# A decoder layer's first projection unit: its weight split moved ahead of the copies of the rows, its halves in two banks, and products that nobody reads ahead of it

## The chip, the cores and the metric

The kernel runs on one core of one Trainium2 chip. The metric is the device time of one execution in microseconds (us): lower is better. Engines are named as in the profile: PE (TensorE), PEld (its weight loads), DVE (VectorE), ACT (ScalarE), POOL (GpSimd), SP (SyncE, which issues nearly all transfers here).

## The reference

A decoder layer over 256 tokens of width 1024, in float32. Only its first line matters for the change; the rest is named to show what follows it.

```python
h = rms_norm(x, norm_mix_g[l])                        # (256, 1024)
proj = jnp.einsum('bsd,dc->bsc', h, w_in[l])          # (1024, 3080) weights
fq, fk, fv, f_logit, mq, mk, mv = jnp.split(proj, splits, axis=-1)
...                                                    # two kinds of attention, 8 heads each
x = x + jnp.einsum('bsc,cd->bsd', mixed, w_out[l])
h = rms_norm(x, norm_ffn_g[l])
x = x + hierarchical_moe(h, ...)                       # 32 experts, 2 a token, 96 MB of weights
return rms_norm(x, norm_final_g)
```

## The kernel before, in words

The program is written engine by engine, each in its own block, with semaphores between them; the order on an engine is the order of the code. No scheduler moves anything.

**Start.** SP issues the loads in this order: the two row tiles of x (512 KB each), four small vectors, the forget gate's weights `wf`, then `w_in` in pieces: two units of 256 columns (1 MB each, line 341), then five blocks of 512 columns (2 MB each, line 350). ACT squares each row tile (line 816), DVE and POOL make its reciprocal root, DVE scales the tile into `xn` (line 1161), and PE transposes its eight 128x128 pieces into banks 4 to 7 (line 469). A bank holds two of the eight slices k of the depth 1024.

**Split in two parts.** Rows and weights are each split for the products: `hi` is the value rounded to the fast matmul format, `lo` is what is left. ACT copies a slice of the transposed rows to `h_hi` (line 861) and DVE makes `h_lo` from the same bank (line 1165). ACT rounds a unit's weights to `unit_hi` (`split_hi`, line 839) and DVE subtracts to get `unit_lo` (`split_lo`, line 1173). For the first unit alone the subtraction is shared: POOL makes the lower four slices (line 1085, semaphore `half_lo_ready`) and DVE the upper four. Both start on the same semaphore, `w_hi_ready`.

**Units.** There are twelve units of 256 columns. A unit is 48 products of 128x256, 24 for each half of 128 columns: eight slices of hi times hi, eight of hi weights with `h_lo`, eight of lo weights with `h_hi`. `unit(0)` and `unit(1)` come first (line 488), then the forget gate (line 573), units 2 to 11 with the attention between them, the output projection, the router, and then the experts in passes, two experts side by side. During the experts SP waits for a pass to release a buffer and then issues the next 1 MB weight loads (lines 360, 367 and 415).

**Banks.** Unit u writes bank u % 3, both halves in one bank, and ACT takes it with one copy of 512 columns (line 823). Bank 3 (`O_BANK`) is first written by the forget gate. The tile `cpart` is a piece of SBUF that DVE sets to zero at the very start (line 1155).

Of the kernel before, what the change touches and what calls it, by code (L numbers as in the profile page):

```python
# [24 lines left out]
P = 128  # L25
SEQ = 256
# [3 lines left out]
KD = D // P  # L30
# [33 lines left out]
def layer_program(nc, I, out):  # L64
# [4 lines left out]
    with ctx:  # L69
# [3 lines left out]
        def sem(name):  # L73
            return ctx.enter_context(nc.semaphore(name))
# [181 lines left out]
        O_BANK = 3  # L256
# [19 lines left out]
        tr_done, h_hi_ready, h_lo_ready = sem("tr_done"), sem("h_hi_ready"), sem("h_lo_ready")  # L276
        w_hi_ready, w_lo_ready, wf_hi_ready, wf_lo_ready = (sem(n) for n in ("w_hi_ready", "w_lo_ready", "wf_hi_ready", "wf_lo_ready"))
        pad_clear = sem("pad_clear")
        grp_done, act_took, dve_took = sem("grp_done"), sem("act_took"), sem("dve_took")
        ft_done, ss_done, sq_ready, half_lo_ready = (sem(n) for n in ("ft_done", "ss_done", "sq_ready", "half_lo_ready"))  # L280
        fz_ready, fa_ready, fl_ready, fc_ready = (sem(n) for n in ("fz_ready", "fa_ready", "fl_ready", "fc_ready"))
# [25 lines left out]
        def grp_bank(g):  # L307
            return bank[g % 3]

        def wait_bank_free(pe, g):  # L310

            if g >= 3:
                if g - 3 < G_OF:
                    pe.wait_ge(act_took, g - 2)
                else:
                    pe.wait_ge(dve_took, g - 3 - G_OF + 1)
# [138 lines left out]
        @block.tensor  # L456
        def _(pe):
            mm = nc.tensor.matmul
            pe.wait_ge(cst_in, 16)

            pe.wait_ge(gv_in, 64)
# [2 lines left out]
            for t in range(NT):  # L464
                pe.wait_ge(xn_ready, t + 1)
                for i in range(KD // 2):
                    for k in (2 * i, 2 * i + 1):
                        c = (k % 2) * SEQ + t * P
                        last = nc.tensor.transpose(bank[4 + i][:, c:c + P], xn[:, t, k * P:(k + 1) * P], ident)
                    if t == NT - 1:  # L470
                        last.then_inc(tr_done, 1)
            def unit(u, parts=(0, 1)):

                if parts[0] == 0:
                    wait_bank_free(pe, u)
                    pe.wait_ge(w_hi_ready, u + 1)
                hi, lo = unit_hi[unit_buf(u)], unit_lo[unit_buf(u)]
                for i in parts:
                    out = grp_bank(u)[:, i * UNIT:(i + 1) * UNIT]  # L480
                    if u < G_FV:
                        for n, (w, h) in enumerate(((hi, h_hi), (hi, h_lo), (lo, h_hi))):
                            if n == 2:
                                wait_split(pe, u)
                            for k in range(KD):
                                if u == 0 and i == 0 and n < 2:
                                    pe.wait_ge((h_hi_ready, h_lo_ready)[n], k + 1)
                                last = mm(out, w[:, k, i * P:(i + 1) * P], h[:, k, :], start=(n == 0 and k == 0), stop=(n == 2 and k == KD - 1))  # L488
                    else:
                        for n, (h, w) in enumerate(((h_hi, hi), (h_lo, hi), (h_hi, lo))):  # L490
                            if n == 2:
                                wait_split(pe, u)
                            for k in range(KD):
                                last = mm(out, h[:, k, i * P:(i + 1) * P], w[:, k, :], start=(n == 0 and k == 0), stop=(n == 2 and k == KD - 1))  # L494
                if parts[-1] == 1:
                    last.then_inc(grp_done, 1)
# [67 lines left out]
                    last.then_inc(grp_done, 1)  # L564

            pe.wait_ge(gcol_set, 1)
            unit(0)
            unit(1)

            pe.wait_ge(wf_lo_ready, 1)  # L570
# [227 lines left out]
        def _(act):  # L798
# [55 lines left out]
                took(g, mqk[:, w, :, c:c + UNIT], both_tiles(g))  # L854

            for k in range(KD):
                if k == KD // 2:
                    split_hi(0)
                act.wait_ge(tr_done, k // 2 + 1)  # L860
                A(h_hi[:, k, :], bank[4 + k // 2][:, (k % 2) * SEQ:(k % 2 + 1) * SEQ], ACT.Copy, scale=gcol[:, k:k + 1]).then_inc(h_hi_ready, 1)
            split_hi(1)
            act.wait_ge(wf_in, 16)
            nc.scalar.copy(wf_hi[:, :, :], wf).then_inc(wf_hi_ready, 1)
            take_qk(0)
            split_hi(2)
            take_qk(1)
            split_hi(3)
# [275 lines left out]
        def _(dve):  # L1144
# [7 lines left out]
                dve.wait_ge(dve_step, steps[0])  # L1152

            V.memset(onescol, 1.0).then_inc(ones_set, 1)
            V.memset(cpart, 0.0)

            for t in range(NT):
                dve.wait_ge(ssq_ready, t + 1)
                V.tensor_scalar(var[:, t:t + 1], ssq[:, t:t + 1], 1.0 / D, EPS, ALU.mult, ALU.add).then_inc(var_ready, 1)
                dve.wait_ge(pow_ready, t + 1)  # L1160
                V.tensor_scalar(xn[:, t, :], x[:, t, :], rstd[:, t:t + 1], None, ALU.mult).then_inc(xn_ready, 1)
            dve.wait_ge(gcol_set, 1)
            for k in range(KD):
                dve.wait_ge(h_hi_ready, 2 * (k // 2) + 2)
                V.scalar_tensor_tensor(out=h_lo[:, k, :], in0=bank[4 + k // 2][:, (k % 2) * SEQ:(k % 2 + 1) * SEQ], scalar=gcol[:, k:k + 1],
                                       in1=h_hi[:, k, :].bitcast(fp32), op0=ALU.mult, op1=ALU.subtract).then_inc(h_lo_ready, 1)

            def split_lo(u):

                dve.wait_ge(w_hi_ready, u + 1)  # L1170
# [1 line left out]
                k = slice(KD // 2 if u == 0 else 0, KD)  # L1172
                V.tensor_tensor(unit_lo[b][:, k, :], unit_src(u)[:, k, :], unit_hi[b][:, k, :].bitcast(fp32), ALU.subtract).then_inc(w_lo_ready, 1)  # L1173

            split_lo(0)
            split_lo(1)
            dve.wait_ge(wf_hi_ready, 1)
            V.tensor_tensor(wf_lo[:, :, :], wf, wf_hi[:, :, :].bitcast(fp32), ALU.subtract).then_inc(wf_lo_ready, 1)
# [330 lines left out]
```

## Time and profile before

| what | us |
|---|---|
| median of 3 runs | 364.67 (364.49 to 366.02) |
| the profiled execution | 363.79 |
| its span, first to last instruction | 361.6 |
| PE busy in the span | 312.5 (86%) |
| mean granted TensorE clock, as a share of 2.4 GHz | 0.978 |

The rows further down are all of the profiled execution, whose own time is 2.2 us above its span and 0.88 us below the median of the runs. Start times count from the first instruction.

### The profile page before, as it was taken

The page shows a single profiled execution, that of the slowest core. Times are in us where ns is not written, and L with a number is a line of the kernel's source. Part 1 is how long each engine was busy: PE and PEld are TensorE (multiplying, and loading weights), DVE is VectorE, ACT ScalarE, POOL GpSimd, SP SyncE. Part 2 cuts the span into 40 slices and gives each one's busy share as a digit, 9 for nine tenths or more (in the row PEclk, how much of TensorE's full clock was granted, in tenths as well). Part 3 has the DMA queues.
Part 4 walks back from the last instruction along what each step waited for, and adds up shares of the span by engine and source line. Part 5 has one row for each costly group of instructions (what it writes and reads, how often), then busy time and mean ns, then how long its engine had stood idle before and what let it go on. Part 6 is the DMA issues. An engine that isn't in the chain of part 4 may idle for free.

```text
span 361.6 us, 11575 instructions
## 1 busy us (share of the span) xinstructions
PE 312.5 (86%) x4740; PEld 240.3 (66%) x4741; DVE 163.9 (45%) x453; ACT 125.0 (35%) x307; POOL 42.7 (12%) x73
## 2 busy tenths in 40 slices
PE   1799999999999989889979898889999999766571
PEld 1699989889875545667657665657677777546250
DVE  2635545383353612774535344435555544341334
ACT  4726336545241426533313232312323323220223
POOL 1200000363402225620000000000000000000002
PEclk9899999999999999999989999999999999998997
DMA  8999795062729989489999999999999999999943
GB/s 254 352 386 387 263 392 239 3 237 112 280 81 400 314 353 387 160 304 348 418 414 357 418 418 414 416 418 410 423 412 421 418 415 423 410 424 416 414 175 116
DMA packets 32652, 121.17 MB, mean 335 GB/s; under 512 B 5497, under 2 KB 7825, under 8 KB 24689
## 3 DMA queue, kind: packets, MB, share of 16 engines
q1 hardware_dynamic: 32480, 120.65, 85.1%
q8 instruction: 21, 0.34, 0.4%
q10 hardware_dynamic: 144, 0.13, 0.1%
q14 instruction: 7, 0.05, 0.0%
HBM read 119.72 MB, written 1.05 MB: 334 GB/s over the span
## 4 chain that ended last, share of the span: by engine, by line
PE 68%; issue 8%; DMA 7%; DVE 4%; DVEq 4%; SPq 4%; ACT 3%; POOL 0%; POOLq 0%; ACTq 0%
PE bank L494 13%; PE bank L770 8%; PE bank L738 7%; PE bank L698 7%; PE bank L561 7%; PE bank L488 7%; DMA spare<-in_w_up_dram 6%; PE bank L705 4%; SPq L360 2%; PE bank L508 2%; PE bank L759 2%; ACT yb L1016 2%; PE bank L523 1%; DVEq L1431 1%; DMA ring<-in_norm_ffn_g_dram 1%
## 5 line engine op out<-in xcount | busy, mean ns | idle before, releaser
L738 PE MATMUL bank<-ring,hT 128*32 128x128 f32 x1664 | 53.2, 279 | 12.7 <-issue 4.7
L738 PEld LDWEIGHTS bank<-ring,hT 128*32 128x32 f32 x1664 | 46.1, 112 | 23.8 <-issue 23.3
L1426 DVE SCALAR_TENSOR_TENSOR yb<-bank,pp,yb 64x512 fp32r<-64x512 f32 x36 | 27.0, 749 | 45.8 <-ACT yb L1016 45.2
L1173 DVE TENSOR_TENSOR unit_lo<-ring,unit_hi 128x2048 fp32r<-128x2048 f32 (+1 forms) x12 | 26.3, 2207 | 32.6 <-ACT unit_hi L839 32.6
L698 PE MATMUL bank<-pp,qk 128*128 128x64 bf16 x912 | 30.6, 194 | 8.2 <-issue 4.7
L698 PEld LDWEIGHTS bank<-pp,qk 128*128 128x128 bf16 x912 | 28.1, 98 | 13.4 <-issue 7.4
L1016 ACT ACTIVATE yb<-bank,pp 64x512 fp32r<-64x512 f32 x36 | 24.6, 683 | 28.9 <-PE bank L770 28.4
L1078 POOL TENSOR_TENSOR stats<-stats 128x1 f32<-128x1 f32 (+1 forms) x7 | 4.6, 664 | 219.8 <-DVE stats L1457 199.7
L561 PE MATMUL bank<-ring,qk 128*128 128x512 f32 (+1 forms) x72 | 29.9, 551 | 0.0
L770 PE MATMUL bank<-ring,pp 128*32 128x512 f32 x208 | 25.0, 598 | 0.0
L705 PE MATMUL bank<-yb,selT 128*128 128x512 f32 x76 | 23.3, 428 | 1.7 <-DVE yb L1426 1.6
L738 PE MATMUL bank<-work,hT 128*32 128x128 f32 x320 | 19.4, 273 | 4.8 <-DMA spare<-in_w_up_dram 2.9
L738 PEld LDWEIGHTS bank<-work,hT 128*32 128x32 f32 x320 | 17.0, 110 | 9.0 <-issue 8.9
L839 ACT CAST unit_hi<-ring 128x2048 fp32r<-128x2048 f32 x12 | 22.8, 1911 | 0.0
L1368 DVE TENSOR_TENSOR hT<-bank,stats 128x256 f32<-128x256 f32 x38 | 14.5, 420 | 14.8 <-PE bank L698 14.8
L1006 ACT ACTIVATE pp<-bank,stats 128x128 f32<-128x128 f32 x18 | 6.6, 368 | 41.0 <-PE bank L738 41.0
L738 PE MATMUL bank<-spare,hT 128*32 128x128 f32 x320 | 19.5, 274 | 0.0
L561 PEld LDWEIGHTS bank<-ring,qk 128*128 128x128 f32 x72 | 12.7, 190 | 9.9 <-issue 9.7
L1008 ACT COPY pp<-bank 128x128 f32<-128x128 f32 x18 | 4.8, 266 | 41.2 <-PE bank L761 41.2
L1398 DVE TENSOR_SCALAR pp<-cf,qk 128x64 f32<-128x64 f32 x76 | 18.6, 309 | 0.0
L494 PE MATMUL bank<-unit_hi,h_hi 128*128 128x256 f32 x128 | 18.4, 287 | 0.0
L494 PE MATMUL bank<-unit_hi,h_lo 128*128 128x256 f32 x128 | 18.0, 283 | 0.0
(197 smaller groups left out, 513.6 us busy)
## 6 DMA issues: line engine op xcount, KB each, us to landing
ring<-in_w_up_dram SPq DMA_DIRECT2D x24, 1024.0 KB, 19.1
ring<-in_w_down_dram SPq DMA_DIRECT2D x24, 1024.0 KB, 19.1
ring<-in_w_gate_dram SPq DMA_DIRECT2D x22, 1024.0 KB, 16.9
ring<-in_w_in_dram SPq DMA_DIRECT2D x5, 2048.0 KB, 19.4
ring<-in_w_out_dram SPq DMA_DIRECT2D x4, 1024.0 KB, 8.5
spare<-in_w_gate_dram SPq DMA_DIRECT2D x4, 1024.0 KB, 19.0
spare<-in_w_up_dram SPq DMA_DIRECT2D x4, 1024.0 KB, 19.7
work<-in_w_gate_dram SPq DMA_DIRECT2D x4, 1024.0 KB, 16.8
```

Source lines behind the costliest of these rows:

```text
L488: last = mm(out, w[:, k, i * P:(i + 1) * P], h[:, k, :], start=(n == 0 and k == 0), stop=(n == 2 and k == KD - 1))
L494: last = mm(out, h[:, k, i * P:(i + 1) * P], w[:, k, :], start=(n == 0 and k == 0), stop=(n == 2 and k == KD - 1))
L561: last = mm(grp_bank(g)[:, 0:w], oT[:, j, t * P:(t + 1) * P], w_o[:, group, c // HALF, k, c % HALF:c % HALF + w], start=(k == 0), stop=(k ...
L698: last = mm(dst[:, k * CP:(k + 1) * CP], hs[i][:, t, k, :], selb[:, t, :], start=(t == 0 and i == 0), stop=(t == NT - 1 and i == 2))
L705: last = mm(acc[t][half][:, :], selT[:, t * P:(t + 1) * P], yb[half][:, :], start=False, stop=final)
L738: last = mm(p_gu[b:b + CAP, w * P:(w + 1) * P], hg[:, k, CAP * e:CAP * (e + 1)], w_gu[at[e]][:, w, k, h, :], start=(k == 0), stop=(k == KD ...
L770: last = mm(p_y[b:b + CAP, :], actT[:, CP * f + CAP * e:CP * f + CAP * (e + 1)], w_dn[at[e]][:, f, h * HALF:(h + 1) * HALF], start=(f == 0 ...
L839: nc.scalar.copy(unit_hi[unit_buf(u)][:, :, :], unit_src(u)).then_inc(w_hi_ready, 1)
L1016: A(yb[half][rows, :], p_y[rows, :], ACT.Copy, scale=wcol[rows, :]).then_inc(y_hi_ready, 1)
L1173: V.tensor_tensor(unit_lo[b][:, k, :], unit_src(u)[:, k, :], unit_hi[b][:, k, :].bitcast(fp32), ALU.subtract).then_inc(w_lo_ready, 1)
L1398: last = V.tensor_scalar(selw[:, t, :].rearrange("p (h e c) -> p e h c", h=2, e=2)[:, e], slots.rearrange("p (h c) -> p h c", h=2), at, we ...
L1426: V.scalar_tensor_tensor(out=yb[half][rest, :], in0=p_y[rows, :], scalar=wcol[rows, :], in1=yb[half][rows, :].bitcast(fp32), op0=ALU.mult, ...
```

## The change

Four things are done to the start of the program; nothing behind unit 1 is edited, except that PE waits before unit 2, which writes bank 2, until ACT has emptied it.

```diff
+        WARM = 20
+        first_bank = [bank[0], bank[2]]
         def wait_bank_free(pe, g):
+            if g == 2:
+                pe.wait_ge(act_took, 1)
...
         @block.tensor
+            pe.wait_ge(zero_set, 1)
+            for i in range(WARM):
+                mm(bank[O_BANK][:, 0:SEQ], cpart[:, 0:P], cpart, start=True, stop=True)
             pe.wait_ge(cst_in, 16)
...
+            def first_unit():
+                pe.wait_ge(w_hi_ready, 1)
+                hi, lo = unit_hi[0], unit_lo[0]
+                for n, (w, h) in enumerate(((hi, h_hi), (lo, h_hi), (hi, h_lo))):
+                    if n == 1:
+                        wait_split(pe, 0)
+                    for k in range(KD):
+                        if n != 1:
+                            pe.wait_ge(h_hi_ready if n == 0 else h_lo_ready, k + 1)
+                        for i in range(2):
+                            last = mm(first_bank[i][:, 0:SEQ], w[:, k, i * P:(i + 1) * P], h[:, k, :],
+                                      start=(n == 0 and k == 0), stop=(n == 2 and k == KD - 1))
+                last.then_inc(grp_done, 1)
...
-            unit(0)
+            first_unit()
             unit(1)
...
         @block.scalar
+            split_hi(0)
             for k in range(KD):
-                if k == KD // 2:
-                    split_hi(0)
                 act.wait_ge(tr_done, k // 2 + 1)
                 A(h_hi[:, k, :], bank[4 + k // 2][:, (k % 2) * SEQ:(k % 2 + 1) * SEQ], ACT.Copy, scale=gcol[:, k:k + 1]).then_inc(h_hi_ready, 1)
...
-            take_qk(0)
+            act.wait_ge(grp_done, 1)
+            for i in range(2):
+                last = nc.scalar.copy(qT[:, i, :], first_bank[i][:, 0:SEQ])
+            last.then_inc(act_took, 1)
...
         @block.vector
-            V.memset(cpart, 0.0)
+            V.memset(cpart, 0.0).then_inc(zero_set, 1)
...
             dve.wait_ge(gcol_set, 1)
+            split_lo(0)
             for k in range(KD):
                 dve.wait_ge(h_hi_ready, 2 * (k // 2) + 2)
                 V.scalar_tensor_tensor(out=h_lo[:, k, :], in0=bank[4 + k // 2][:, (k % 2) * SEQ:(k % 2 + 1) * SEQ], scalar=gcol[:, k:k + 1],
                                        in1=h_hi[:, k, :].bitcast(fp32), op0=ALU.mult, op1=ALU.subtract).then_inc(h_lo_ready, 1)
-            split_lo(0)
             split_lo(1)
```

On PE, the first unit of before stands in these rows behind the transposes; `unit_hi_53` and `unit_lo_57` are the first unit's weight parts, `unit_hi_54` is the second unit's.

```order
L488 MATMUL bank<-h_hi,unit_hi_53 128x256 [waits h_hi_ready,w_hi_ready,gcol_set]
L488 MATMUL bank<-h_hi,unit_hi_53 128x256 [waits h_hi_ready] x7
L488 MATMUL bank<-h_lo,unit_hi_53 128x256 [waits h_lo_ready] x8
L488 MATMUL bank<-h_hi,unit_lo_57 128x256 [waits w_lo_ready,half_lo_ready]
L488 MATMUL bank<-h_hi,unit_lo_57 128x256 x7
L488 MATMUL bank<-h_hi,unit_hi_53 128x256 x8
L488 MATMUL bank<-h_lo,unit_hi_53 128x256 x8
L488 MATMUL bank<-h_hi,unit_lo_57 128x256 [waits w_lo_ready,half_lo_ready]
L488 MATMUL bank<-h_hi,unit_lo_57 128x256 x7
L488 MATMUL bank<-h_hi,unit_hi_54 128x256 [waits w_hi_ready]
```

With the change the same place reads as follows, from the last pair of hi times hi products to the first pair with `h_lo` (seven more hi pairs stand ahead, the first of which also waits for `w_hi_ready`, and seven more `h_lo` pairs behind).

```order
L494 MATMUL bank<-h_hi,unit_hi_53 128x256 [waits h_hi_ready]
L494 MATMUL bank<-h_hi,unit_hi_53 128x256
L494 MATMUL bank<-h_hi,unit_lo_57 128x256 [waits w_lo_ready,half_lo_ready]
L494 MATMUL bank<-h_hi,unit_lo_57 128x256 x15
L494 MATMUL bank<-h_lo,unit_hi_53 128x256 [waits h_lo_ready]
L494 MATMUL bank<-h_lo,unit_hi_53 128x256
```

So each slice of `h_hi` now feeds two products as it comes, 16 products need the rows' hi parts alone, and the wait for the weights' lo parts stands behind those 16 instead of behind 8 hi and 8 `h_lo` products; 32 products are left behind that wait in either order.

On ACT, the rows of before from the copy of the gains to the first unit's result:

```order
L818 COPY gcol<-bank 128x24 [waits gcol_t]
L861 ACTIVATE h_hi<-bank,gcol 128x256 [waits tr_done,gcol_set]
L861 ACTIVATE h_hi<-bank,gcol 128x256 [waits tr_done] x3
L839 CAST unit_hi_53<-ring 128x2048 [waits unit_in0]
L861 ACTIVATE h_hi<-bank,gcol 128x256 [waits tr_done] x4
L839 CAST unit_hi_54<-ring 128x2048 [waits unit_in1]
L864 CAST wf_hi<-ring 128x64 [waits wf_in]
L823 COPY qk<-bank 128x512 [waits grp_done]
```

The same stretch of ACT with the change:

```order
L842 COPY gcol<-bank 128x24 [waits gcol_t]
L863 CAST unit_hi_53<-ring 128x2048 [waits unit_in0,gcol_set]
L884 ACTIVATE h_hi<-bank,gcol 128x256 [waits tr_done] x8
L863 CAST unit_hi_54<-ring 128x2048 [waits unit_in1]
L887 CAST wf_hi<-ring 128x64 [waits wf_in]
L890 COPY qk<-bank 128x256 [waits grp_done]
L890 COPY qk<-bank 128x256
```

The rounding of the first weights, which stood between the fourth and the fifth copy of the rows, now stands ahead of all eight.

On DVE, the rows of before around the first lo parts:

```order
L1161 TENSOR_SCALAR pp<-work,stats 128x1024 [waits pow_ready]
L1165 SCALAR_TENSOR_TENSOR h_lo<-bank,gcol,h_hi 128x256 [waits h_hi_ready,gcol_set]
L1165 SCALAR_TENSOR_TENSOR h_lo<-bank,gcol,h_hi 128x256 [waits h_hi_ready] x7
L1173 TENSOR_TENSOR unit_lo_57<-ring,unit_hi_53 128x1024 [waits w_hi_ready]
L1173 TENSOR_TENSOR unit_lo_58<-ring,unit_hi_54 128x2048 [waits w_hi_ready]
```

The same stretch of DVE with the change:

```order
L1187 TENSOR_SCALAR pp<-work,stats 128x1024 [waits pow_ready]
L1193 TENSOR_TENSOR unit_lo_57<-ring,unit_hi_53 128x1024 [waits w_hi_ready,gcol_set]
L1199 SCALAR_TENSOR_TENSOR h_lo<-bank,gcol,h_hi 128x256 [waits h_hi_ready] x8
L1193 TENSOR_TENSOR unit_lo_58<-ring,unit_hi_54 128x2048 [waits w_hi_ready]
L1204 TENSOR_TENSOR wf_lo<-ring,wf_hi 128x64 [waits wf_hi_ready]
```

DVE's half of the first weights' lo part moved ahead of the eight `h_lo` slices, so that it and POOL's half wait for nothing but the same `w_hi_ready`.

## Rows read from the trace of the kernel before

**Rows 1.** Pieces of the chain that ended last: start us, us, what.

```profile
7.61 3.67 PE bank L469 x16
11.29 2.28 issue
13.56 13.97 PE bank L488 x96
27.53 2.78 PE bank L573 x24
...
187.81 1.53 PE bank L705 x4
...
197.13 0.93 PE bank L705 x4
...
321.94 21.78 DMA spare<-in_w_up_dram
```

**Rows 2.** Timeline of the start: start us, us, engine, line, what, count, idle before it.

```profile
10.11 1.57 ACT L861 ACTIVATE h_hi<-bank,gcol 128x256 fp32r<-128x256 f32 x4 [2.31 <-PE bank L469]
11.55 1.91 ACT L839 CAST unit_hi<-ring 128x2048 fp32r<-128x2048 f32 x1
13.34 1.60 ACT L861 ACTIVATE h_hi<-bank,gcol 128x256 fp32r<-128x256 f32 x4
13.54 2.39 POOL L1085 TENSOR_TENSOR unit_lo<-ring,unit_hi 128x1024 fp32r<-128x1024 f32 x1 [5.29 <-ACT unit_hi L839]
14.24 1.66 DVE L1165 SCALAR_TENSOR_TENSOR h_lo<-bank,gcol,h_hi 128x256 fp32r<-128x256 f32 x4 [1.53 <-ACT h_hi L861]
15.37 1.91 PE L488 MATMUL bank<-h_lo,unit_hi 128*128 128x256 f32 x8
17.18 1.72 PE L488 MATMUL bank<-h_hi,unit_lo 128*128 128x256 f32 x8
18.74 1.12 PE L488 MATMUL bank<-h_hi,unit_hi 128*128 128x256 f32 x8
21.61 1.12 PE L488 MATMUL bank<-h_hi,unit_hi 128*128 128x256 f32 x8
```

**Rows 3.** Landings, of lines 341 (two loads) and 350 (five): issued, and us to landing.

```profile
L341 SPq DMA_DIRECT2D ring<-in_w_in_dram x2: 582/1232/1883, 3.5 to 4.1; - x2
DMA to landing us min/median/max: 6.5/7.8/9.0
L350 SPq DMA_DIRECT2D ring<-in_w_in_dram x5: 437/4008/6372, 9.3 to 21.7; - x5
DMA to landing us min/median/max: 10.7/19.4/20.8
```

**Rows 4.** POOL and DVE alone, 69.5 to 75.5 us; then line 1067's durations (ns min/median/max).

```profile
72.64 2.45 POOL L1067 TENSOR_TENSOR ring<-qk 128x256 f32<-128x256 f32 x1 [0.24 <-ACT qk L903]
72.32 2.29 DVE L1173 TENSOR_TENSOR unit_lo<-ring,unit_hi 128x2048 fp32r<-128x2048 f32 x1 [3.74 <-ACT unit_hi L839]
L1067 POOL TENSOR_TENSOR ring<-qk x6: 609/614/2446, 72.6 to 117.4; 128x256 f32<-128x256 f32 x6
L1173 DVE TENSOR_TENSOR unit_lo<-ring,unit_hi x12: 1220/2292/2326, 15.8 to 89.4; 128x2048 fp32r<-128x2048 f32 x11, 128x1024 fp32r<-128x1024 f32 x1
```

**Rows 5.** Stretches: us, PE busy (count), PE clock granted, DMA share, GB/s.

```profile
15.00:16.00 1.00, 1.00 (x5) 0.50 1.03 385
19.00:20.00 1.00, 1.00 (x11) 1.00 1.05 387
148.00:152.00 4.00, 2.82 (x16) 1.00 0.19 41
184.00:188.00 4.00, 3.41 (x56) 0.70 1.00 418
192.00:196.00 4.00, 4.00 (x140) 1.00 0.78 280
```

**Rows 6.** Longest waits of SP's queue: for whom, us in total, times, longest.

```profile
SPq L360 <- PE bank L738: 23.6, 13, 13.0
```

More of the change, by code:

```diff
@@ L278, in layer_program @@
         pad_clear = sem("pad_clear")
+        zero_set = sem("zero_set")
         grp_done, act_took, dve_took = sem("grp_done"), sem("act_took"), sem("dve_took")
@@ L485, in unit @@
                             for k in range(KD):
-                                if u == 0 and i == 0 and n < 2:
-                                    pe.wait_ge((h_hi_ready, h_lo_ready)[n], k + 1)
                                 last = mm(out, w[:, k, i * P:(i + 1) * P], h[:, k, :], start=(n == 0 and k == 0), stop=(n == 2 and k == KD - 1))
@@ L1161, in _ @@
                 V.tensor_scalar(xn[:, t, :], x[:, t, :], rstd[:, t:t + 1], None, ALU.mult).then_inc(xn_ready, 1)
[L1162 to L1166, printed above, removed]
             def split_lo(u):
@@ L1173, in split_lo @@
                 V.tensor_tensor(unit_lo[b][:, k, :], unit_src(u)[:, k, :], unit_hi[b][:, k, :].bitcast(fp32), ALU.subtract).then_inc(w_lo_ready, 1)
+            dve.wait_ge(gcol_set, 1)
             split_lo(0)
+            for k in range(KD):
+                dve.wait_ge(h_hi_ready, 2 * (k // 2) + 2)
+                V.scalar_tensor_tensor(out=h_lo[:, k, :], in0=bank[4 + k // 2][:, (k % 2) * SEQ:(k % 2 + 1) * SEQ], scalar=gcol[:, k:k + 1],
+                                       in1=h_hi[:, k, :].bitcast(fp32), op0=ALU.mult, op1=ALU.subtract).then_inc(h_lo_ready, 1)
             split_lo(1)
```

## The prediction

> **What bounds the kernel now.** I read the chain of waits first, since it says which stretch of the start is worth anything. It runs on PE almost without a break from the transposes on, and the only long piece of it that is no engine's work is the last weight load, 21.78 us from its issue to its landing at 343.7 [rows 1]. At the start the chain has one hole: PE ends the transposes at 11.3, stands still for 2.28 us, and then runs 96 products of line 488 without a stop that the chain names, 13.97 us [rows 1]. At full clock 96 would take 11.5: eight products last 1.12 us there, which is seven steps and a last one of 0.28, so a step is 0.12 [rows 2]. So the first unit has two places to gain: the hole, and 2.5 us of slack inside.
>
> The timeline shows both. ACT copies four slices of the rows, rounds the first weights from 11.55, and only when they are done, at about 13.48, can PE begin; then it copies the other four, and PE follows at the copies' pace of 0.36 us (four in 1.60: three steps and 0.51). The eight `h_lo` products from 15.37 take 1.91 and the next eight from 17.18 take 1.72, steps of 0.21 instead of 0.12 [rows 2]; the stretch view has the granted clock at 0.50 there, that is 1.2 GHz, and back at 1.00 at 19 [rows 5]. PE had stood still ahead of 13.5 and worked in short pieces behind it. The second unit starts at 21.61 [rows 2]. This is the mark of the whole calculation: how much earlier does it start?
>
> **Step 1, the weights first.** The first unit's 1 MB is issued at 3.5 and lands 6.5 later, at 10.0 [rows 3]. That is the moment at which ACT now starts its first copy (10.11 [rows 2]), so the moved rounding starts at 10.05. In the rows the next copy starts 1.79 behind its start (13.34 less 11.55), and the semaphore comes at 1.92; so hi weights at 11.97, and eight copies from 11.84 on in steps of 0.36: the first is ready at 11.84 + 0.51 = 12.35, the last at 11.84 + 7 x 0.36 + 0.51 = 14.87. Before, the last was ready at 14.94 by the same sum (13.34 + 1.60). ACT's work is only put in another order, so the rows are not ready sooner; what changes is that PE can follow the copies from the first on. What ACT had as cover, its copies between the landing and 11.55, is gone: from here on the landing of the first weights is on the path, one for one.
>
> **Step 2, both halves at each slice.** PE starts at 12.4 and has two products, 0.24 us, for every 0.36. Its last pair starts at 14.9 and is through at 15.15. At half clock the pair would take 0.43, so 16 would take 3.4 and end at 15.8: PE then sets the pace, and the bound is 0.65 worse.
>
> **Step 3, the lo weights.** Now 32 products are left, all behind the wait for both halves of the lo part. DVE's half took 1.2 us in the rows of its line, POOL's 2.39 [rows 2, 4]. Side by side they would be ready at 12.0 + 2.4 = 14.4 and hidden behind the pairs. But the trace has one place where such a pair meets. At 72.32 DVE starts a subtraction with both inputs in SBUF, for 2.29 us; POOL starts a product from SBUF 0.3 later and takes 2.45 where the same form takes 0.61, so it ended at 75.09, 0.48 behind DVE's end at 74.61 [rows 4]. It did next to nothing until DVE was done. Against that, POOL ran its half of before beside the `h_lo` instructions in 2.39 [rows 2], and these have one input in a bank. The change makes the bad pair: both halves start on one semaphore at 12.0. One waits for the other, whichever is first: 12.0 + 1.2 + 2.39 = 15.6. PE restarted 0.14 behind the last release before (DVE's half, from 15.82 for 1.22, to 17.18 [rows 2, 4]), so it goes on at 15.74, and stands still for some 0.6.
> The Trainium skill says the same as a rule (SBUF — State Buffer, section Who interferes with whom): a VectorE instruction with two SBUF inputs and a GpSimd instruction that reads SBUF use one port pair, and the second to start blocks until the first is done. By that rule as by the row the sum is 15.74; without it, it would be 15.15. The trace agrees, with 2.45 against 0.61.
>
> **Step 4, the rest of the unit.** 32 steps of 0.12 are 3.84, so the second unit starts at 15.74 + 3.84 = 19.58 instead of 21.61: 2.03 earlier. In parts: the restart behind the lo wait moves from 17.18 to 15.74, 1.44, with 32 products behind it both times; and the eight from 17.18 took 1.56 to the next eight at 18.74, instead of 0.96, which gives 0.60 if the clock holds. I take it that it does: PE works from 12.4 with two thirds of its time filled, where it had stood still until 13.56. Bounds of the start: 1.44 if there is nothing to win back from the clock, 2.62 if the two halves don't block (21.61 less 15.15 + 3.84 = 18.99). I take 2.03, with the row that shows the block and the clock of this trace.
>
> **What costs nothing, and under which cover.** The 20 unread products wait only for DVE's second instruction; at 0.21 each they take 4.3 us, and the transposes don't start before 7.6 [rows 1]. Whether they make the transposes faster has no effect: the last transposes end at 11.3 [rows 1] even at the slow pace, and ACT needs the first pair of slices at 11.84. `h_lo` on DVE starts behind its 1.2 us, at 13.2, and goes in steps of 0.39, limited by the copies: all eight are ready by 16.4, the first is needed at 15.74 + 1.92 = 17.7. If POOL is the first of the two, DVE's half ends at 15.6 and `h_lo` 0 at 16.1: still in time. The second unit's lo part is done 2.3 us behind 16.8, needed at 21.5. ACT's two copies of 256 columns instead of one of 512 cost it some 0.15, eight us ahead of unit 2, which starts at 30.3 less 2.0 [rows 1]; its block of weights lands at 9.3 + 10.7 = 20.0 and the last block at 21.7 + 20.8 = 42.5 [rows 3], both ahead of their use. The new wait ahead of unit 2 is for copies that ended 8 us before.
>
> **Does the start carry to the end?** The end is set by the weight stream, which is full to the last load. But a stream that has run dry starts again when PE releases a buffer, and it runs dry at 148 to 152 (41 GB/s) and again for part of 192 to 196 (280 GB/s) [rows 5]. SP's longest wait for PE in that part, 13.0 us, ends just there [rows 6]. From 196 on it is full. Everything between 42 and 193 is thus released by PE, and moves with it. So the sum is 363.79 - 2.03 = 361.8 for the profiled execution. That one lies 0.88 below the median of the runs, so for the median 364.67 - 2.03 = 362.6. Since part of the runs may not have the 0.60 in them, I say 362.7.
>
> **The rivals.**
> - *Only the wait is won* (2 in 10): the clock's 0.60 is not there in most executions, or comes back as a slow stretch elsewhere in the unit. 1.44 is left: 363.2, within 0.5%.
> - *The halves don't block* (1 in 10): the start gives 2.62, so 362.1. For it speaks only that both are short; the row at 72.6 speaks against.
> - *The stream takes it* (1 in 10): the gaps of 148 to 152 and 192 to 196 close, and the end waits for bytes alone; 364.7, no change. Against it: the first gap alone is nearly four us, more than the shift.
> - *The clock among the experts falls otherwise* (1 in 10): there the granted clock is 0.70 in 184 to 188, and four products of line 705 take 1.53 instead of 0.93 [rows 1, 5], on the way to the release at 193. Another position of such a stretch gives or takes at most 4 x 0.30 = 1.2 there: 361.4 to 363.8.
> - *Slower* (under 1 in 10): the first weights land late. ACT now waits for them with all the rows behind it. Break even is a landing at 12.05 instead of 10.0; if they land with the unit behind them, at 4.1 + 9.0 = 13.1 [rows 3], the start loses 3.1 and wins 2.0: 365.8; it is slower by 0.5% from 13.9 on. For it: both loads share the queues. Against: before, they landed 3.1 apart.
> - *The unread products do nothing.* This is what I expect of them, and it costs nothing.
>
> **How the numbers follow.** 0.5% is 1.8 us, about what a measurement of this kernel can tell from no change. The likeliest case (5 in 10), 2.03 with a spread of some 0.4 for the landing and the clock, lies just over that bound, and two thirds of it count as faster; with the unblocked case and half of the clock case that makes 0.50. The rest of these, the case of the wait alone and that of the stream make 0.43 for no difference, the last rival and what I have not thought of 0.07 for slower. The range goes from 361.3 (unblocked, with luck in the clock among the experts) to 364.4 (nearly all lost on the way).
>
> **What would show it.** In the changed kernel's trace: the rounding of the first weights on ACT starts at the landing, near 10.0; PE's first pair at 12.4 and pairs every 0.36; on POOL the half takes 3.6 instead of 2.4, or DVE's half that much longer, and PE stands still from 15.15 to 15.7; granted clock 1.00 from 15 to 19; the second unit at 19.6; the gap in the stream near 191 instead of 193. The prediction is wrong if the first weights land later than 10.5, if the clock is at 0.50 behind 15, or if the last landing stays at 343.7.

## The result and the profile after

The changed kernel takes 367.0 us in the median (twelve executions), the kernel before beside it 364.2. The ratio of their times is 1.0065, with a 95% interval of 1.0041 to 1.0090: **slower by 0.65%, 2.4 us**, where 362.7 and a gain of 2.0 had been predicted. (All ratios here and below leave out executions over 1.5% above their kernel's fastest: four of these twelve, from 370.8 up, and in e10 three, one of them of 1,044 us.) The profiled execution took 366.56, its span is 364.7 and its mean granted clock 0.970; before they were 363.79, 361.6 and 0.978.

The start did what was predicted. The timeline of the changed kernel, as in [rows 2]:

```profile
9.94 1.90 ACT L863 CAST unit_hi<-ring 128x2048 fp32r<-128x2048 f32 x1 [2.37 <-DMA ring<-in_w_in_dram]
11.75 3.02 ACT L884 ACTIVATE h_hi<-bank,gcol 128x256 fp32r<-128x256 f32 x8
11.92 2.38 POOL L1111 TENSOR_TENSOR unit_lo<-ring,unit_hi 128x1024 fp32r<-128x1024 f32 x1 [3.52 <-ACT unit_hi L863]
11.95 3.43 DVE L1193 TENSOR_TENSOR unit_lo<-ring,unit_hi 128x1024 fp32r<-128x1024 f32 x1 [2.77 <-ACT unit_hi L863]
12.36 2.97 PE L494 MATMUL bank<-h_hi,unit_hi 128*128 128x256 f32 x16 [1.15 <-ACT h_hi L884]
15.52 2.15 PE L494 MATMUL bank<-h_hi,unit_lo 128*128 128x256 f32 x16 [0.20 <-DVE unit_lo L1193]
17.51 2.08 PE L494 MATMUL bank<-h_lo,unit_hi 128*128 128x256 f32 x16
19.43 1.12 PE L512 MATMUL bank<-h_hi,unit_hi 128*128 128x256 f32 x8
```

The second unit's first product, the last row, starts at 19.43, not at 21.61 as in [rows 2]: 2.18 earlier (2.03 predicted). So the profiled execution lacks nearly 5 us against its forecast (366.56 for 361.8), and they were lost later. The chain of waits (start us, us, what) says where:

```profile
3.48 6.38 DMA ring<-in_w_in_dram
9.94 1.91 ACT unit_hi L863
11.95 3.44 DVE unit_lo L1193
15.52 4.07 PE bank L494 x32
19.59 5.76 PE bank L512 x48
...
150.94 4.35 PE bank L684 x6
...
264.44 6.53 issue
270.97 3.58 PE bank L762 x64
```

Two pieces are new. The second of them is long: PE ends a pass at 264.44 and starts the next one at 270.97, and in between it waits for nothing that the profile shows. The last weight load, 21.78 us of the chain before [rows 1], is not in it any more: from 270.97 on the chain goes over PE, with short steps of ACT and DVE between the passes, and over no load. Stretches of the changed kernel (columns: us, PE busy, PEld, DVE, ACT, POOL with counts, PE clock granted, DMA share, GB/s):

```profile
152.00:156.00 4.00, 4.00 (x12) 1.49 (x10) 2.33 (x14) 0.00 (x0) 1.57 (x6) 0.64 0.65 254
...
264.00:268.00 4.00, 0.44 (x6) 0.00 (x0) 1.50 (x2) 1.36 (x2) 0.00 (x0) 0.94 1.00 398
268.00:272.00 4.00, 1.03 (x20) 1.06 (x24) 0.53 (x3) 0.00 (x0) 0.00 (x0) 0.50 1.04 420
```

In 264 to 272 PE is busy for 1.5 of 8 us; the granted clock drops to 0.50 during the stop and is still there when PE goes on (0.50 in 268 to 272), while the DMA engines stay full: it is not data that is late. What is late is on another queue. Transfers of the stretch 255 to 345 us by queue (packets, MB, share of 16 engines), first the changed kernel, then the kernel before:

```profile
q1 hardware_dynamic: 6603, 37.30, 101.0%
q8 instruction: 9, 0.15, 0.7%
```

```profile
q1 hardware_dynamic: 6678, 37.57, 101.7%
```

`q8 instruction` carries PE's code, in packets of 16 KB; that it is PE's shows in e4 and e7 below, where 240 more PE instructions bring one packet more in all, 23 instead of 22. Before, PE fetches none in this stretch; the changed kernel fetches nine, the first at 264.68, where PE has just stopped, the second at 266.37, then one every 6 to 8 us until 310.6. The place is the end of the first of three iterations of the expert loop, where PE jumps back to the loop's first instruction (its branch is at 262.87; the next ones at 313.82 and 352.33). Before, with branches at 260.15, 298.58 and 349.31, the same jump costs a gap of 0.72 us.

From these times the loss can be laid out. The start's 2.19 us are carried by SP's issues up to 151. Then 1.4 is lost to a stretch of half clock over the router's products (150.94 to 155.3, six of them in 4.35 us, and 0.64 in the row of 152 to 156), 1.35 more by SP's issue at 193 (nearly all of it a pause of PE in the products of line 794 at 176: 3.19 us from 175.39, where before they took 1.90), and at the jump PE is 2.7 late.

The 2.2 us between 193 and the jump stand in two more pauses that the kernel before doesn't have, 1.2 at 220 and 0.9 at 252.7; each comes right behind a code packet (217.70 and 250.78), but no run isolates them, and other traces with the stop reach the jump earlier (e2 at 260.41, e3 at 260.91).

The second iteration, with the stop, takes 50.9 us instead of 38.4, 12.5 more: 5.8 at the jump (6.53 for 0.72), 2.3 and 1.2 in stops at 286.35 and 299.68, 1.6 for 64 products at half clock (3.58 for 1.96), and the rest in pieces. The third takes 38.5 instead of 50.7, 12.2 less. The sum of 2.7, 12.5 and -12.2 is 3.0, by which the end comes later.

What the third iteration has less is waiting for weights. PE's longest waits in 260 to 350 (for whom, us in total, times, longest), before and after:

```profile
PE bank L738 <- DMA ring<-in_w_up_dram: 4.6, 2, 2.9
PE bank L738 <- DMA ring<-in_w_gate_dram: 3.1, 1, 3.1
PE bank L738 <- DMA spare<-in_w_up_dram: 2.9, 1, 2.9
PE bank L738 <- DMA spare<-in_w_gate_dram: 1.6, 1, 1.6
PE bank L738 <- issue: 1.4, 2, 0.7
```

```profile
PE bank L762 <- issue: 10.4, 7, 6.5
...
PE bank L722 <- issue: 1.2, 1, 1.2
```

The 12.2 us of waits for loads are gone, all of them: they were PE's slack against the stream, and the wait for code and the half clock behind it have used them up. Without that slack PE sets the end and not the last load, which lands 1.6 us later than before (345.3 for 343.7).

### The profile page after: what moved, and what is told of

Same layout as the page of the kernel before. It is cut to its first block, busy times and chain, and to the rows that moved or that the text cites. A ratio compares the mean times of both kernels' runs of the same rounds, so it can differ in the third digit from the quotient of the medians.

```text
span 364.7 us, 11616 instructions
## 1 busy us (share of the span) xinstructions
PE 320.8 (88%) x4760; PEld 242.4 (66%) x4761; DVE 166.0 (46%) x453; ACT 125.0 (34%) x308; POOL 42.7 (12%) x73
## 4 chain that ended last, share of the span: by engine, by line
PE 73%; issue 10%; DVE 4%; ACT 4%; DVEq 4%; DMA 2%; SPq 1%; POOLq 0%; POOL 0%; ACTq 0%
PE bank L518 13%; PE bank L794 10%; PE bank L762 9%; PE bank L722 8%; PE bank L585 7%; PE bank L729 5%; PE bank L512 5%; PE bank L783 2%; PE bank L532 2%; ACT yb L1042 2%; DMA ring<-in_w_in_dram 2%; PE bank L684 1%; PE bank L547 1%; DVEq L1457 1%; DVEq L1456 1%
## 5 line engine op out<-in xcount | busy, mean ns | idle before, releaser
L1193 DVE TENSOR_TENSOR unit_lo<-ring,unit_hi 128x2048 fp32r<-128x2048 f32 (+1 forms) x12 | 28.6, 2390 | 31.7 <-ACT unit_hi L863 31.7
L722 PEld LDWEIGHTS bank<-pp,qk 128*128 128x128 bf16 x912 | 28.6, 99 | 12.5 <-DVE pp L1373 6.7
L794 PE MATMUL bank<-ring,pp 128*32 128x512 f32 x208 | 28.1, 599 | 0.5 <-issue 0.5
## 6 DMA issues: line engine op xcount, KB each, us to landing
ring<-in_w_down_dram SPq DMA_DIRECT2D x24, 1024.0 KB, 16.9
```

The lines of the kernel that those rows point to most:

```text
L722: last = mm(dst[:, k * CP:(k + 1) * CP], hs[i][:, t, k, :], selb[:, t, :], start=(t == 0 and i == 0), stop=(t == NT - 1 and i == 2))
L794: last = mm(p_y[b:b + CAP, :], actT[:, CP * f + CAP * e:CP * f + CAP * (e + 1)], w_dn[at[e]][:, f, h * HALF:(h + 1) * HALF], start=(f == 0 ...
```

## The experiments

Rivals: the time of the products or the clock after them; the two-bank order or the earlier start, which changes what PE meets at the loop; a part of the start that costs.

**e1_no_products.** The changed kernel without its unread products.

```diff
-            pe.wait_ge(zero_set, 1)
-            for i in range(WARM):
-                mm(bank[O_BANK][:, 0:SEQ], cpart[:, 0:P], cpart, start=True, stop=True)
```

> The changed kernel without the 20 unread products and the wait ahead of them; all else as changed. Theory A (code loading): the 20 products and their weight loads are 40 instructions ahead of the expert loop, and they push the loop over one more loaded block of code, so that its first jump back waits for code (6.5 us at 264 in the changed kernel, and nine more code packets on queue 8). Without them the count of instructions ahead of the loop is that of before: no code packets between 251 and 350 us, no stop of over 3 us near 264, and the start's 2.0 us reach the end: 361.5 to 362.8. Rival B (clock): the start's 2.2 us shift makes PE stand still at a worse moment in the router, 0.50 granted at 151.5, and that eats it: the stretch is still there and the time is 363.5 to 366. Rival C (start): the unread products keep the clock up for the first unit, and without them it runs at half clock: the second unit starts at 20.5 or later instead of 19.4.

Measured: 362.09 beside 363.79, ratio 0.9955 (0.9927 to 0.9984): **faster**. The jump back in its chain, and no row of `q8` between 255 and 345:

```profile
260.75 0.71 issue
```

The rest of the change is thus worth 0.45%, and the products cost 1.0065 against 0.9955, 1.1% or 4.0 us. The interval of the 0.45% goes from 0.6 to 2.7 us. In its profiled execution, which at 364.39 is the second slowest of the twelve, PE ran at half clock up to about 16.9 (its products go in steps of 0.21 until there), and the second unit started 1.42 earlier than before rather than 2.18:

```profile
12.35 3.75 PE L491 MATMUL bank<-h_hi,unit_hi 128*128 128x256 f32 x16 [1.01 <-ACT h_hi L881]
15.90 2.53 PE L491 MATMUL bank<-h_hi,unit_lo 128*128 128x256 f32 x16
...
20.19 1.12 PE L509 MATMUL bank<-h_hi,unit_hi 128*128 128x256 f32 x8
```

**e2_before_products.** The kernel before with the 20 products and nothing else of the change.

```diff
+            pe.wait_ge(zero_set, 1)
+            for i in range(20):
+                mm(bank[O_BANK][:, 0:SEQ], cpart[:, 0:P], cpart, start=True, stop=True)
             pe.wait_ge(cst_in, 16)
...
-            V.memset(cpart, 0.0)
+            V.memset(cpart, 0.0).then_inc(zero_set, 1)
```

> The kernel before with the 20 unread products alone, in the same place, behind DVE's zeroing. Theory A (code loading): the first jump back of the expert loop stops PE for some 6 us and nine more code packets are loaded, so 366.5 to 369, 2 to 5 us slower than before. Rivals B (clock in the router) and C (products help the start): no such stop, 363 to 364.5, since the start is otherwise the old one and the products lie in idle time.

Measured: ratio 1.0125 (1.0081 to 1.0170). The stop is there, and so are nine code packets (0.15 MB of `q8` between 255 and 345). In its chain:

```profile
261.98 6.58 issue
```

Neither the new order nor the earlier start is needed for it. In this trace the second unit started 0.40 later than before, at 22.01: the products brought no clock either.

**e3_20_small.** The same number of unread products, each as small as can be: they take hardly any time of PE's array, but as many instructions.

```diff
-                mm(bank[O_BANK][:, 0:SEQ], cpart[:, 0:P], cpart, start=True, stop=True)
+                mm(bank[O_BANK][0:32, 0:1], cpart[:, 0:32], cpart[:, 0:1], start=True, stop=True)
```

> The changed kernel with its 20 unread products made small (32 weight columns, one column streamed), so that they take a few tenths of their time but are still 40 instructions. Theory A (code loading): as slow as the changed kernel, 365 to 368, with the stop at the first jump back. A theory by which the products' work (clock, power) is what costs: as fast as without them, 361.5 to 363.

Measured: ratio 1.0063 (1.0032 to 1.0094), the same as the change, with the stop:

```profile
262.48 6.68 issue
```

They were over at 1.76 us. The products' work plays no part; it is enough that they are 40 instructions.

**e4_120_small.** 120 small products instead of 20: 240 instructions.

```diff
-            for i in range(WARM):
-                mm(bank[O_BANK][:, 0:SEQ], cpart[:, 0:P], cpart, start=True, stop=True)
+            for i in range(120):
+                mm(bank[O_BANK][0:32, 0:1], cpart[:, 0:32], cpart[:, 0:1], start=True, stop=True)
```

> The changed kernel with 120 small unread products in place of the 20, which is 240 instructions instead of 40. The extra code packets are of 16 KB, 256 instructions of 64 bytes. Theory A (code loading): 240 is nearly a whole packet, so the loop lies in its packets as without any of them, 16 instructions further ahead: no stop at the jump, no packets between 251 and 350 us, 361.5 to 363.5 although there are six times as many instructions (they may delay the transposes by up to 1 us, of which little reaches the end). A theory by which any added instruction costs: slower than the kernel with 20, over 366.

Measured: ratio 0.9995 (0.9973 to 1.0017); no stop (a gap of 0.71 at 259.70) and no code packet in 255 to 345. Six times as many instructions and no stop: it is the place of the code, not its amount. The gain of e1 wasn't there in full, though. Its chain starts like this:

```profile
3.48 7.52 DMA ring<-in_w_in_dram
...
11.08 1.90 ACT unit_hi L863
...
13.50 0.55 PE bank L494
```

The first weights land at 11.00 instead of 9.86, and PE's first product starts at 13.50 instead of 12.36: 1.14 and 1.14, one for one. A code packet runs at 5.53, and SP's two issues take 3.43 us instead of 2.55; that this packet delays the weights is a guess that no run isolates, and e12, without a packet there, has 2.91.

**e7_20_and_100.** The changed kernel's 20 products and 100 small ones behind them, again 240 instructions.

```diff
+            for i in range(100):
+                mm(bank[O_BANK][0:32, 0:1], cpart[:, 0:32], cpart[:, 0:1], start=True, stop=True)
             pe.wait_ge(cst_in, 16)
```

> The changed kernel with its 20 unread products and 100 small ones behind them: 240 instructions ahead, as with 120 small ones. Theory A: no stop at the jump. This leaves the one question what the 20 do for the clock: if keeping PE at work from 1.0 to 5.2 us helps the first unit, this is 0.5 us or more faster than 120 small ones (363.6), 362.5 to 363; if the clock at 12 to 17 us does not depend on them, 363.2 to 364.

Measured: ratio 0.9975 (0.9954 to 0.9995), no stop. The jump back in its chain:

```profile
257.51 0.72 issue
```

The change as it is, with more useless instructions in it, is 0.9% faster than without them.

**e6_behind.** The kernel before with 20 small unread products behind the loop, at the end of PE's program.

```diff
+            for i in range(20):
+                mm(p_gu[0:32, 0:1], cb[:, 0:32], cb[:, 0:1], start=True, stop=True)
```

> The kernel before with 20 small unread products (40 instructions) at the very end of PE's program, behind the expert loop, where the last results are being scaled. Theory A (where the loop lies in the code packets): the same 40 instructions cost nothing here, no code packets between 251 and 350 us, within 0.3% of before (some 2 us of them lie beside the last steps of DVE and ACT). If the number of instructions in all were what counts, 365.5 to 368.

Measured: ratio 0.9991 (0.9965 to 1.0017), no stop (0.72 at 260.60). Behind the loop the 40 instructions cost nothing.

**e8_10_products** and **e11_16_products.** The changed kernel with fewer products, one execution each.

```diff
-        WARM = 20
+        WARM = 10
```

> The changed kernel with 10 unread products, 20 instructions instead of 40. Read for the code packets alone: theory A has a step somewhere between 0 and 40 instructions, so this trace has either none of the nine packets between 251 and 350 us and no stop near 262, or all of them and a stop of 6 to 7 us, and nothing between. A cost that grows with the instructions would give a stop of about half, 3 us.

```diff
-        WARM = 20
+        WARM = 16
```

> The changed kernel with 16 unread products instead of 20, that is 32 instructions ahead instead of 40 (10 products, 20 instructions, left the expert loop without a stop). If the cost is a step set by where the loop's code lies, it is there in whole, 6.5 us and nine code packets, or not at all; a cost that grows with the instructions would show a stop of 2 to 5 us. The run tells on which side of 32 instructions the step lies.

Measured: 363.98 and 365.55. The jump back in the chain of the first and of the second:

```profile
264.05 0.71 issue
```

```profile
261.46 6.72 issue
```

20 instructions: no stop, no packet. 32: the whole stop and nine packets. 40: the same. The stop is a step; what it costs in whole time, two single executions can't say.

**e5_one_lo.** e1 with the shared port's block taken away: DVE makes all eight slices of the first unit's lo part, and POOL's instruction and the wait for it are out.

```diff
-            nc.gpsimd.tensor_tensor(unit_lo[0][:, k, :], unit_src(0)[:, k, :], unit_hi[0][:, k, :].bitcast(fp32),
-                                    ALU.subtract).then_inc(half_lo_ready, 1)
...
-                k = slice(KD // 2 if u == 0 else 0, KD)
+                k = slice(0, KD)
```

> The kernel without the unread products, with DVE making all eight slices of the first unit's lo weights and POOL none; its wait is gone with its instruction. Theory of the shared port (two SBUF inputs on DVE beside a POOL instruction that reads SBUF): in the changed kernel DVE's half lasts 3.43 us instead of 1.2 because it waits for POOL's; alone, DVE needs 2.3 for the double work, so the lo weights are ready at 14.3 instead of 15.4, before PE has done the 16 hi products, and PE goes through without the stop of 0.4: the second unit starts 0.35 to 0.45 earlier, 361.2 to 362 in all. If the long DVE instruction came from something else (the transfers, the copies on ACT), it would stay over 3 us for 2048 elements, the lo weights would come later than now, and the time would be 362 to 363.

Measured: ratio 0.9955 (0.9926 to 0.9983). DVE's subtractions (ns min/median/max), and PE's rows:

```profile
L1184 DVE TENSOR_TENSOR unit_lo<-ring,unit_hi x12: 2281/2292/2328, 11.9 to 86.7; 128x2048 fp32r<-128x2048 f32 x12
```

```profile
12.31 2.96 PE L489 MATMUL bank<-h_hi,unit_hi 128*128 128x256 f32 x16 [1.12 <-ACT h_hi L879]
15.11 2.07 PE L489 MATMUL bank<-h_hi,unit_lo 128*128 128x256 f32 x16
18.94 1.12 PE L507 MATMUL bank<-h_hi,unit_hi 128*128 128x256 f32 x8
```

Alone, DVE does the double work in 2.29 us, where its half took 3.43 beside POOL's. PE no longer stops ahead of the lo products, and the second unit starts at 18.94, 0.49 earlier than in the changed kernel. In the whole time the 0.49 can't be told from e1.

**e9_weights_first.** The kernel before with the order on ACT and DVE alone.

```diff
+            split_hi(0)
             for k in range(KD):
-                if k == KD // 2:
-                    split_hi(0)
...
             dve.wait_ge(gcol_set, 1)
+            split_lo(0)
             for k in range(KD):
...
-            split_lo(0)
             split_lo(1)
```

> The kernel before with one part of the change alone: on ACT the first weights are rounded ahead of the eight copies of the rows, and on DVE the half of their lo part stands ahead of h_lo. PE's program is untouched, and there are no unread products, so no theory expects a stop at the first jump back of the expert loop. By the changed kernel's trace DVE's half then ends at about 15.4 us beside POOL's half, h_lo begins there, and its eight slices come every 0.39 from about 15.9 to 18.6. PE's first half of the unit meets them behind its eight hi products, which follow the copies until about 15.1: it ends its h_lo products at 18.8, and has 8 + 24 products of 0.12 left, 3.8 us: the second unit at 22.6 instead of 21.61, 1.0 later. If the order on ACT and DVE alone carried the gain, it would start some 2 us earlier instead. Whole time: 364.5 to 365 by the first, 362 by the second.

Measured: ratio 1.0106 (1.0072 to 1.0140): slower, as by the first reading, and by more. Its timeline:

```profile
11.95 3.41 DVE L1166 TENSOR_TENSOR unit_lo<-ring,unit_hi 128x1024 fp32r<-128x1024 f32 x1 [2.92 <-ACT unit_hi L839]
12.36 3.04 PE L488 MATMUL bank<-h_hi,unit_hi 128*128 128x256 f32 x8 [1.08 <-ACT h_hi L860]
15.81 3.32 PE L488 MATMUL bank<-h_lo,unit_hi 128*128 128x256 f32 x8 [0.41 <-DVE h_lo L1172]
...
20.64 1.84 PE L488 MATMUL bank<-h_hi,unit_hi 128*128 128x256 f32 x8
24.23 1.12 PE L488 MATMUL bank<-h_hi,unit_hi 128*128 128x256 f32 x8
```

The block on DVE pushes `h_lo` behind 15.3, and in the old order PE needs `h_lo` right behind the hi products. The eight `h_lo` products end near 18.9 as expected; then the steps are 0.21 up to 22.3, which adds 1.6, and the second unit starts at 24.23, 2.6 later than before. The whole loses 3.9 us, 1.3 more than that; this trace also has the granted clock at 0.50 from 155 to 159 and from 189.5 to 196, and no run says whose doing that is.

**e10_pairs_only.** The other part alone: two banks and the new order on PE, ACT and DVE as before, no unread products.

```diff
-            split_hi(0)
             for k in range(KD):
+                if k == KD // 2:
+                    split_hi(0)
...
-            split_lo(0)
             for k in range(KD):
...
+            split_lo(0)
             split_lo(1)
```

> The other part alone: both halves side by side in two banks and PE's new order of products, with ACT and DVE in the order of before (rounding between the fourth and the fifth copy, DVE's half behind h_lo), and no unread products, so no stop in the expert loop. PE starts at 13.5 as before, is through with its 16 hi products at 15.3, waits for DVE's half until 17.2 (15.82 and 1.22, and 0.14), and then has 32 products at 0.12, 3.84 us: the second unit at 21.0 instead of 21.61, 0.6 earlier. If the pairs alone carried the gain, it would start at 19.6. Whole time: 363.2 to 363.6 by the first, 362 by the second.

Measured: ratio 1.0035 (0.9996 to 1.0074), no gain, and not clearly a loss. Its timeline, and one stretch of it:

```profile
13.41 2.92 PE L491 MATMUL bank<-h_hi,unit_hi 128*128 128x256 f32 x16 [2.28 <-issue]
17.02 3.75 PE L491 MATMUL bank<-h_hi,unit_lo 128*128 128x256 f32 x16 [0.69 <-DVE unit_lo L1191]
...
22.79 1.12 PE L509 MATMUL bank<-h_hi,unit_hi 128*128 128x256 f32 x8
```

The restart at 17.02 was expected at 17.2. But the granted clock is at 0.50 from 15 to 21 in the stretches of this trace, and the 32 products behind the wait take 5.8 us and not 3.84; the second unit starts 1.2 later than before, not 0.6 earlier. How much of the whole time is the order's and how much this clock's, the run doesn't tell apart. Neither part gains alone: weights first needs PE's new order, to have work that doesn't ask for `h_lo`, and PE's new order needs the weights first, to start before 13.4.

**e12_one_lo_10.** e5 with 10 unread products, 20 instructions.

```diff
+            pe.wait_ge(zero_set, 1)
+            for i in range(10):
+                mm(bank[O_BANK][:, 0:SEQ], cpart[:, 0:P], cpart, start=True, stop=True)
```

> The candidate: the changed kernel with 10 unread products instead of 20, and the whole lo part of the first weights made by DVE (POOL's instruction and its wait are out). 10 products with their weight loads are 20 instructions, which left the loop's code where it does no harm, so no stop of PE at the first jump back (a gap of about 0.7 us). DVE's subtraction takes 2.3 us from 11.9, done at 14.2 as without the products. If the products do nothing but take instructions, the whole time is that of the same kernel without them, 0.9955 of before, 362.4 to 362.9. If they win clock in the first unit in most executions (up to 1.2 us, the difference between the starts of the runs so far), it is 0.992 to 0.994, 361.5 to 362. If 20 instructions move the loop badly in this program, it is 1.006 as for the change.

Measured: 362.14, ratio **0.9938** (0.9912 to 0.9964), faster than both kernels, with a gap of 0.71 at the jump. Its interval overlaps that of e5, so that the products win something is not shown; and in its profiled execution they didn't hold the clock (16 lo products in 2.70 us, the second unit at 20.73).

## Why the prediction was wrong

**The step that failed** is "What costs nothing, and under which cover". It asked only when the 20 products run and who waits for them, and there it was right. It didn't ask where their 40 instructions put the code behind them, and so put them at nothing. What stands in its place: they cost 4.0 us in the whole (e1 against the change), through a stop of 6.5 us at the loop's first jump back and shorter ones behind it. e2 shows that they alone do it, e3 that their time doesn't matter, e6 that it needs them ahead of the loop, e4, e7, e8 and e11 that it is a question of position. The Trainium skill (Runtime: NRT & Kernel Launch, Instruction fetch mechanics) bears on it: code comes in 16 KiB blocks of 256 instructions into a memory that has 128 KiB for PE, and a taken branch whose target isn't in the current window of two pages waits for a fetch.
The stop was not of the order of one fetch either: the first took 1.02 us, the second was fetched at 266.37, and PE went on at 270.97. My theory of a loop that lies over one packet more than PE keeps is not shown either, and the third iteration speaks against it: code that doesn't fit would be fetched in every iteration, but in the changed kernel the third, with the same code at the same place, fetched nothing (no packet between 310.57 and 351.36). Which packet the first jump waits for, and why 32 instructions are enough and 20 and 240 are not, the runs don't show beyond the position itself.

**"Does the start carry to the end?"** failed as well. It followed the weight stream alone, and took it for given that PE has slack against it. It has, 12.2 us of waits for loads behind the jump, and that is why a second iteration 12.5 us longer costs only 4.0 in the whole. But the slack doesn't cover all of it. Where there is no stop, the path of this section was right: in e1's trace the second unit starts 1.42 earlier than before and SP's issue at 193 comes 1.58 earlier (191.41 for 192.99). The rival of a clock that falls otherwise was seen, though not where I put it: over the router's products at 151, in the trace of the change and in those of e9 and e10, and in none of the other ten experiments.

**Step 1** held: the landing at 9.86 (10.0 predicted), PE's first product at 12.36 (12.4). That the landing is on the path one for one is shown by e4, 1.14 for 1.14.

**Step 2** held: the last pair is through at 15.3 (15.15).

**Step 3** held in its sum, PE going on at 15.52 (15.74), but the engine that is blocked is DVE, 3.43 us for a half that took 1.22 [rows 4], and not POOL (2.38). e5 shows the cause by taking POOL's half away. The rule cited there from the Trainium skill (SBUF — State Buffer, Who interferes with whom) was right, the order included: POOL starts at 11.92 and DVE at 11.95, and it is the second that is held up.

**Step 4** held in the profiled execution, 2.18 for 2.03, and nearly so in its split, 1.66 for the restart (17.18 to 15.52; 1.44 predicted) and 0.52 for the clock (0.60). That the clock's part came was luck: it differs from trace to trace, also with the same start. The second unit started 1.42 earlier in e1 and 1.39 in e3, with half clock up to 16.9 in both, and 2.67 in e5. The timed gain without the products is 0.45% or 1.6 us, which lies between "only the wait is won" (1.44) and the likeliest case (2.03), and is near both.

**The rivals.** The slower side had under 1 in 10, for a late landing of the first weights; the price per us was right, and the case didn't come. None of the rivals was the one that came, and the range didn't reach it. The chances were also added up wrongly: by their own terms those of a gain make 0.48 and those of no difference 0.52, not 0.50 and 0.43.

## What to carry to other kernels

Ahead of a long loop in an engine's program every added instruction is a change to where the loop's code lies, whether it does work or not. Compare the rows of the instruction queue between the two profiles, and look at the engine's gap at each jump back; if there is a new stop of several us with nothing waited for, add or drop some instructions ahead of the loop before judging the rest of the edit. Here the same start runs at 1.0065 with the twenty products and at 0.9955 without them. Ten of them brought no stop, and with the lo part made by DVE alone that kernel runs at 0.9938. And an order of work on one engine can't be judged alone: by themselves the two parts of this start showed no gain (1.0035) and a loss (1.0106), and together a gain (0.9955).

## What the runs showed of the hardware

- A loop of PE of some 1,720 recorded instructions runs its second and third iteration without one code packet, or with nine of 16 KB and a stop of 6.5 to 6.7 us at the first jump back, depending on whether 0, 20 or 240 or else 32 or 40 instructions are added ahead of it. The nine lie within the second iteration (264.68 to 310.57); the third is quiet again.
- PE's pauses with nothing waited for also stand next to code packets where it runs the code for the first time, in the kernel before too: 2.54 us at 224.54 with a packet at 224.50. That the packet is their cause is not shown.
- Two subtractions from SBUF on DVE and POOL, started 0.03 us apart: POOL's took 2.38, as alone, and DVE's 3.43 instead of 1.22. The same double work on DVE alone took 2.29. Here, sharing it between the two engines cost 1.1 us.
- Dense work did not bring PE's clock back soon in every trace: in e10 the granted clock stayed at 0.50 from 15 to 21, the last four us of it with products without a gap (from 17.02), in e5 products at the same place ran at full speed. Unread products ahead didn't decide it: with 20 of them the first unit ran at full clock in the change and at half clock in e2, and with none at full clock in e5 and at half clock in e1.
- In e9 the stretches from 19 to 22 name a granted clock of 1.00, while the products there go in steps of 0.21, the pace of half clock (0.12 at full clock). Near the start go by the steps and not by the column.
